# A retention, convolution and expert layer: the work ahead of the gather loop in another order

## The chip, the core and the metric

One NeuronCore of a Trainium2 chip runs the whole program. The metric is the device time of one execution in microseconds. TensorE is PE in the profile, VectorE is DVE, ScalarE is ACT, GpSimd is POOL, and SyncE is SP, which here only issues DMAs.

## The reference, cut to what matters

```python
h = rmsnorm(x)                                    # 512 prompt rows and 32 rows of running streams, D = 1024
q, k, v, g, a, b = split(h @ w_in)                # six sections of 512 columns
u = a * sigmoid(b)                                # gated
c = depthwise_conv(concat(conv_buf, u), 31 taps)  # per channel, 512 channels
y_conv = silu(layer_norm(c + bias) * gain + bias2)
o = retention(rotary(q), rotary(k), v, state)     # 4 heads of 128
y_ret = silu(g) * group_norm(o) * gain
x = x + concat(y_ret, y_conv) @ w_out
h = rmsnorm(x)
for each of 8 heads:                              # experts by product keys
    scores = (h @ query) against 2 x 128 keys; the best 16 of each; the best 16 of the 256 sums
    x += sum over 16 of softmax(best) * gelu(h . down[expert]) * up[expert]
y = rmsnorm(x)
```

Everything is in float32. `down` and `up` rows lie side by side, so an expert is one row of 8 KB.

## The kernel before

**Tiles.** The 544 rows are five tiles: four of 128 (tiles 0 to 3) and the sample tile of 32 (`SAMPLE`, tile 4). The 8 heads and the tiles make 34 virtual tiles (`VT`): for each head four of 128 rows, and the sample rows of all heads folded into two more. Each virtual tile gathers 16 experts for each of its 128 rows, 16 DMAs of 128 rows (`gathers`, L460), 544 in all.

**Front, on PE.** The normalised rows are transposed (`norm_t`, L1059). Sections A and B (`glu`) are computed channel-major: 32 pairs of products with 512 and with 32 columns each (L1077, L1082). Sections Q, K, G and V are row-major, one product of 8 matmuls for each tile (`qkvg`, L1090; a float32 matmul shows as two records). Then come the means and variances of the convolution's channels (`ln_mean`, `ln_var`, L1104), retention tile by tile (`ret_qT`, `ret_kT`, `ret_scores`, `ret_out`, `ret_state`, `ret_yT`), and the output product of each tile in two halves (`mix_out`, L1090 again). A weight section has 2 MB and a ring of three places in SBUF; SP loads the next when PE has drained the section whose place it takes.

**Front, on the others.** ACT empties the section products. DVE waits for all of section B and then computes 31 taps over four channel groups, each in a 512-column and a 32-column instruction, a drain after each tap (L728). GpSimd rotates q and k of a tile with twelve operations of 256 elements (L441 to L444); for tile 0 that starts when K's first product is in SBUF, which is during the taps. DVE copies the transposed heads, normalises retention's output with a root from GpSimd (`retention_root`, L424), and adds the output products to `xs` (`mix_add`, L833).

**Routing.** When a tile's two output halves are added, ACT squares it, GpSimd takes the root (`mixed_root`), DVE normalises (`peer_norm`, L853), PE turns it (`ffn_t`) and computes queries and scores (L1189, L1201), and DVE finds the best keys (`top_first`, `top_second`) and the experts (`top_sums`, L898, whose last line L918 releases the gathers). For head 0 this is done tile by tile in `TRANSITION`; later heads are done for all tiles at once beside the sums, from L1217 on.

**Expert loop.** The 11 ring places of gathered rows lie in the same SBUF as the weight ring and the sections' results, so the first gathers must wait until those are free. For each group of four experts DVE computes the dot products (`weigh`, L933), ACT makes gelu, weights and four diagonal matrices (L620 to L630), and PE sums the `up` rows through them (`sum_up`, L1246), which frees the four places.

**What sets the order.** Each engine's program is in order and written out by hand. PE's order is `retention_schedule` and `TRANSITION`. Each PE job has a PSUM bank, numbered round: seven banks, and three (4 to 6) from `ffn_t` of tile 2 on, because the sums use banks 0 to 3. A job waits until the engine that empties the former job of its bank has done so (`open_bank`, L1039; `BEFORE`).

## Time and profile before

| | us |
|---|---|
| median of 3 runs | 1797.5 (1796.53 to 1797.82) |
| the profiled execution | 1796.54 |
| its span in the trace | 1794.6 |
| PE busy | 1522.6 |
| DVE busy | 1171.6 |
| GpSimd busy | 744.8 |
| ACT busy | 496.4 |

The span is what the trace covers; the profiled execution's own time is 1.9 us longer. The page divides the span into 40 equal slices of 44.9 us. A busy PE is not PE at its peak, because matmuls are pipelined. PEclk is the granted clock as a share of 2.4 GHz.

### The profile page before, as it was taken

The numbers are of one execution on the slowest core, as the hardware profiler recorded it, in microseconds if no ns is written. First come the engines' busy times: TensorE is split into PE (matmuls) and PEld (weight loads), VectorE is DVE, ScalarE is ACT, GpSimd is POOL, SyncE is SP. The second block draws the span as 40 slices with busy tenths as digits, with TensorE's granted clock in tenths as the row PEclk, the third lists the DMA queues.
The fourth block names the chain that finished last, engine by engine and source line by source line (L and its number), as shares of the span: only waits on it lengthen the run. The fifth ranks groups of instructions, "written<-read, shape, count | busy, mean of one in ns | idle before, by whom it ended". The sixth has DMA issues, their size and how long they took to land.

```text
span 1794.6 us, 14135 instructions
## 1 busy us (share of the span) xinstructions
PE 1522.6 (85%) x4008; PEld 700.3 (39%) x4008; DVE 1171.6 (65%) x2667; ACT 496.4 (28%) x1562; POOL 744.8 (42%) x654
## 2 busy tenths in 40 slices
PE   7999979968988978997798889788977988777887
PEld 3544345534433433342244334333423443332332
DVE  2089863357567767766766777677677677777655
ACT  1000110122332333332333323333333332333332
POOL 1002144133254545453554544444454445455452
PEclk9899989989999999998999999999999999899899
DMA  5112100288999999999999999999999999999996
GB/s 221 47 58 83 62 1 1 68 341 329 362 404 421 421 421 421 422 421 422 421 402 423 422 420 401 422 421 389 408 422 421 421 421 422 421 421 410 421 416 248
DMA packets 84847, 605.53 MB, mean 337 GB/s; under 512 B 10880, under 2 KB 11136, under 8 KB 13088
## 3 DMA queue, kind: packets, MB, share of 16 engines
q0 software_dynamic: 78336, 570.46, 77.1%
q1 hardware_dynamic: 6432, 34.16, 5.0%
q8 instruction: 32, 0.52, 0.1%
q14 instruction: 47, 0.39, 0.1%
HBM read 601.31 MB, written 2.88 MB: 337 GB/s over the span
## 4 chain that ended last, share of the span: by engine, by line
DMA 39%; PE 38%; DVE 13%; ACT 4%; issue 2%; POOL 1%; DVEq 1%; ACTq 1%; POOLq 0%; SPq 0%
DMA arena<-experts,expert 38%; PE ps L1246 21%; DVE region_b L728 6%; PE ps L1217 5%; PE ps L1090 5%; DVE arena L933 5%; PE ps L1077 3%; ACT weight L623 2%; ACT diag L630 1%; PE ps L1082 1%; PE ps L1189 1%; POOL arena L465 1%; PE ps L1104 1%; ACT gl L620 1%; ACTq L625 1%
## 5 line engine op out<-in xcount | busy, mean ns | idle before, releaser
L1246 PE MATMUL ps<-arena,diag 128*128 128x512 f32 x2176 | 1031.2, 631 | 234.1 <-ACT diag L630 233.9
L465 POOL DMA_INDIRECT arena<-experts,expert x544 | 669.3, 1230 | 760.3 <-PE ps L1246 672.4
L933 DVE CUSTOM_DVE_ANT_0 arena<-arena,hn 128x1024 f32<-128x1024 f32 x544 | 654.8, 1222 | 365.9 <-DMA arena<-experts,expert 361.4
L1246 PEld LDWEIGHTS ps<-arena,diag 128*128 128x128 f32 x2176 | 428.8, 201 | 818.9 <-issue 603.4
L620 ACT ACTIVATE gl<-dots 128x4 f32<-128x4 f32 x136 | 27.9, 205 | 801.4 <-DVE dots L933 801.4
L630 ACT ACTIVATE diag<-cst,weight 128x128 f32<-128x128 f32 x544 | 173.8, 390 | 9.6 <-issue 0.3
L1090 PE MATMUL ps<-arena,hT 128*128 128x512 f32 (+1 forms) x320 | 145.9, 616 | 1.0 <-issue 1.0
L623 ACT ACTIVATE weight<-gl,gate 128x1 f32<-128x1 f32 x544 | 115.8, 283 | 9.9 <-issue 0.7
L728 DVE SCALAR_TENSOR_TENSOR region_b<-region_b,par 128x512 f32<-128x512 f32 x240 | 108.0, 521 | 2.7 <-issue 0.5
L1217 PE MATMUL ps<-hT,region_b 128*128 128x512 f32 x224 | 98.5, 593 | 0.4 <-issue 0.4
L441 POOL TENSOR_TENSOR hn<-arena,cst 128x256 f32<-128x256 f32 (+1 forms) x20 | 16.2, 808 | 193.5 <-ACT arena L529 127.0
L1090 PEld LDWEIGHTS ps<-arena,hT 128*128 128x128 f32 (+1 forms) x320 | 56.9, 181 | 86.8 <-issue 86.8
L1090 PE MATMUL ps<-arena,region_b 128*128 128x512 f32 (+1 forms) x160 | 70.5, 594 | 0.0
L1217 PEld LDWEIGHTS ps<-hT,region_b 128*128 128x128 f32 x224 | 42.5, 190 | 53.5 <-issue 53.5
L1077 PE MATMUL ps<-hT,arena 128*128 128x512 f32 x128 | 58.5, 619 | 2.8 <-DVE hT L707 2.5
L713 DVE SCALAR_TENSOR_TENSOR region_b<-region_b 128x512 f32<-128x512 f32 x4 | 2.5, 686 | 75.8 <-ACT region_b L517 75.8
L944 DVE TENSOR_TENSOR xs<-ps,xs 128x1024 f32<-128x1024 f32 (+1 forms) x34 | 41.4, 1219 | 15.3 <-PE ps L1246 15.3
L933 DVE DVE_READ_ACCUMULATOR2_ANT dots<- 128x1 f32 x544 | 44.5, 82 | 0.0
L620 ACT ACT_TABLE_LOAD x34 | 43.6, 1283 | 0.6
L606 ACT ACT_TABLE_LOAD x33 | 42.3, 1283 | 1.7
L1090 PEld LDWEIGHTS ps<-arena,region_b 128*128 128x128 f32 (+1 forms) x160 | 27.0, 174 | 36.8 <-issue 36.5
L529 ACT ACTIVATE arena<-ps 128x512 f32<-128x512 f32 (+1 forms) x15 | 8.9, 595 | 110.7 <-PE ps L1090 110.7
(125 smaller groups left out, 845.1 us busy)
## 6 DMA issues: line engine op xcount, KB each, us to landing
arena<-weights SPq DMA_DIRECT2D x8, 2048.0 KB, 8.9
...
arena<-experts,expert POOLq DMA_INDIRECT x544, 14.9
...
```

Source lines behind the costliest of these rows:

```text
L465: pool.indirect_dma_start(rows_of(n), None, experts, bass.IndirectOffsetOnAxis(ap=expert[:, vt % BUFS, k:k + 1], axis=0))\
L606: nc.scalar.activation(gate[:, u, :], best_s[:, u, :], ACT.Exp, bias=neg_max[:, u:u + 1], accum_out=gate_sum[:, u:u + 1]).then_inc(s_exp, 1)
L620: nc.scalar.activation(gl[:, vt % 2, ks], dots[:, vt % 2, ks], ACT.Gelu_apprx_tanh)
L623: nc.scalar.activation(weight[:, vt % 2, k:k + 1], gl[:, vt % 2, k:k + 1], ACT.Copy, scale=gate[:, vt % BUFS, k:k + 1])
L630: nc.scalar.activation(diag[:, n % DIAGS, :], base, ACT.Copy, scale=weight[:, vt % 2, k:k + 1])\
L728: last = v.scalar_tensor_tensor(out=out, in0=src[:, c, j:j + n], scalar=tap, in1=out, op0=ALU.mult, op1=ALU.add)
L933: last = v.tensor_tensor_reduce(out=rows_of(n)[:, 0:D], in0=rows_of(n)[:, 0:D], in1=hn[:, tile_of(vt)], scale=1.0, scalar=0.0, op0=ALU.mul ...
L944: v.tensor_tensor(out=xs[0:rows, tile], in0=total, in1=xs[0:rows, tile], op=ALU.add).then_inc(s_acc, 1)
L1077: last = mm(out, w[:, k, c * P:(c + 1) * P], hT[:, k, 0:SEQ], start=k == 0, stop=k == KD - 1)
L1090: last = mm(out[0:r, :], lhs[:, k, lo:lo + r], w[:, k, :], start=k == 0, stop=k == KD - 1)
L1217: last = mm(out, weights[:, k, i * KEYS:(i + 1) * KEYS], hT[:, k, 0:SEQ], start=k == 0, stop=k == KD - 1)
L1246: last = mm(ps[:, 2 * (vt % 2) + half, :], diag[:, n % DIAGS, :], rows_of(n)[:, D + half * SEC:D + (half + 1) * SEC], start=k == 0, stop=k ...
```

## The change

- PE's whole order, front and transition, is one list (`plan`). Sections A and B are computed in token halves of 272 columns, channel groups 0 and 1 first and then 2 and 3. Tile 3 and the sample tile are transposed after the first two half products. One product of G stands ahead of the means, one ahead of the variances, three behind them.
- The four channel groups' rows lie in one buffer of 604 columns, prompt and sample together, so a tap is one instruction of 574 columns. DVE does the 31 taps of groups 0 and 1, then those of groups 2 and 3, with a drain after each pair. The normalisation of the channels is done in two blocks of tokens, 128 and 416.
- GpSimd rotates in place, q and k together, six operations of 512 elements for a tile, after the last tap (`s_conv`), all tiles in a row.
- Retention, the output product and the routing of tile 0 come before the retention of tiles 2 to 4; the output products of the others follow. ACT instead of DVE copies the transposed heads and the turned-back output.
- PSUM: eight banks, and four (4 to 7) from `ffn_t` of tile 0 on.
- The ring places have another order, since gathers can start before the last sections are through; the number of places, 11, stays.
- SP issues the loads in another order: tile 3 and the sample rows behind section A; head 0's query weights when the taps are done; the gain of the second norm twice, once for tile 0 into its own place. The waits on PE's drains are waits on single PE jobs.

```diff
+EXT = PAD + SEQ + PAD + DEC
+WIDE = EXT - PAD
+HALF = T // 2
+BLOCKS = ((0, P), (P, T))
...
+    late = [(c, i) for c in (2, 3) for i in range(2)]
+    order = turn("norm_t", 0) + turn("norm_t", 1) + turn("norm_t", 2) + glu(S_A, (0, 0), (1, 0)) + turn("norm_t", 3)
+    order += turn("norm_t", SAMPLE) + glu(S_A, (0, 1), (1, 1)) + glu(S_B, (0, 0), (0, 1), (1, 0), (1, 1))
+    order += glu(S_A, *late) + glu(S_B, *late) + rows(S_Q, *range(TILES)) + rows(S_K, *range(TILES)) + rows(S_G, 0)
+    order += blocks("ln_mean") + rows(S_G, 1) + blocks("ln_var") + rows(S_G, 2, 3, SAMPLE)
+    order += rows(S_V, 0) + head(0) + rows(S_V, 1) + scores(0) + head(1) + out(0) + rows(S_V, 2) + scores(1) + back(0)
+    order += mix(0, 0) + out(1) + head(2) + mix(0, 1) + scores(2) + back(1) + rows(S_V, 3) + turn("ffn_t", 0)
+    order += query(0) + keys(0) + out(2) + head(3) + rows(S_V, SAMPLE) + scores(3) + mix(1, 0) + back(2) + mix(1, 1)
+    order += out(3) + head(4) + scores(4) + turn("ffn_t", 1) + query(1) + keys(1) + back(3) + out(4) + mix(2, 0)
+    order += back(4) + mix(2, 1) + sums(0, 0) + mix(3, 0) + turn("ffn_t", 2) + query(2) + mix(3, 1) + sums(0, 1)
+    order += keys(2) + mix(4, 0) + turn("ffn_t", 3) + query(3) + sums(0, 2) + mix(4, 1) + keys(3) + sums(0, 3)
+    return order + turn("ffn_t", 4) + query(4) + sums(1, 0) + keys(4) + sums(1, 1)
...
+BANKS = 8
+SUM_BANKS = 4
+Q_BANKS = SUM_BANKS
+FIRST_SUM = JOB[("ffn_t", 0, 0)]
+BANK = {name: n % BANKS if n < FIRST_SUM else SUM_BANKS + (n - FIRST_SUM) % (BANKS - SUM_BANKS)
+        for name, n in JOB.items()}
+BEFORE = {name: [other for other in JOBS[:n] if BANK[other] == BANK[name]][-1:] for name, n in JOB.items()}
...
+OPENING = [0, 1, 2, 3, 4, 5, 6, 0, 1, 2, 3, 7, 8, 9, 10]
+CYCLE = [4, 5, 6, 0, 1, 2, 3, 7, 8, 9, 10]
+SLOT = OPENING + [CYCLE[n % SLOTS] for n in range(VT * TOPK - len(OPENING))]
+PLACE = [6, 7, 4, 5, 8, 9, 10, 0, 1, 2, 3]
...
+            x_rows(0)
             sp.dma_start(cst[:, C_IDENT:], consts[:, C_IDENT:]).then_inc(s_ident, 16)
             sp.dma_start(par[:, :], params).then_inc(s_par, 16)
...
+            x_rows(1)
+            x_rows(2)
+            weight_rows(S_A)
+            x_rows(3)
+            x_rows(SAMPLE)
+            weight_rows(S_B)
+            weight_rows(S_Q)
+            sp.dma_start(u[:, :, PAD + SEQ:PAD + SEQ + PAD], conv_state).then_inc(s_st, 16)
+            sp.dma_start(state[:, 1], state_ret).then_inc(s_st, 16)
+            sp.dma_start(cst[:, 0:C_IDENT], consts[:, 0:C_IDENT]).then_inc(s_cst, 16)
+            sp.wait_ge(s_pe, JOB[("glu", S_A, CT - 1, 1)] + 1)
+            weight_rows(S_K)
+            sp.wait_ge(s_pe, JOB[("glu", S_B, CT - 1, 1)] + 1)
+            weight_rows(S_G)
+            sp.wait_ge(s_pe, JOB[("qkvg", S_Q, SAMPLE)] + 1)
+            weight_rows(S_V)
+            sp.wait_ge(s_u, 1)
+            sp.dma_start(conv_prompt, u[:, :, SEQ:SEQ + PAD]).then_inc(s_convout, 16)
+            sp.dma_start(conv_sample, u[:, :, EXT - PAD:EXT]).then_inc(s_convout, 16)
+            sp.wait_ge(s_pe, JOB[("qkvg", S_K, SAMPLE)] + 1)
+            weight_rows(S_OUT)
+            sp.wait_ge(s_convout, 32)
+            sp.wait_ge(s_conv, 1)
             sp.dma_start(head_flat[0], head_weights[0]).then_inc(s_hw[0], 16)
+            sp.wait_ge(s_pe, JOB[("qkvg", S_G, SAMPLE)] + 1)
+            weight_rows(S_OUT + 1)
+            sp.wait_ge(s_rot, TILES)
+            sp.dma_start(first_gain, gain_ffn.to_broadcast([P, D])).then_inc(s_gain1, 16)
+            sp.wait_ge(s_yconv, len(BLOCKS))
+            sp.dma_start(row_gain, gain_ffn.to_broadcast([P, D])).then_inc(s_gain, 16)
+            sp.wait_ge(s_by["dve"], EMPTIED[("ret_state", SAMPLE)])
...
+            def rotary(t):
+
+                r = ROWS[t]
+                pool.wait_ge(s_by["act"], EMPTIED[("qkvg", S_K, t)])
+                src = z[0:r, t, S_Q:S_K + 1].rearrange("p s (h d) -> p (s h) d", d=HD)
+                x1, x2 = src[:, :, 0:half], src[:, :, half:HD]
+                cos = trig[0:r, t, 0].unsqueeze(1).to_broadcast([r, 2 * HEADS, half])
+                sin = trig[0:r, t, 1].unsqueeze(1).to_broadcast([r, 2 * HEADS, half])
+                nc.gpsimd.tensor_tensor(out=rot[0][0:r], in0=x2, in1=sin, op=ALU.mult)
+                nc.gpsimd.tensor_tensor(out=rot[1][0:r], in0=x1, in1=sin, op=ALU.mult)
+                pool.drain()
+                nc.gpsimd.tensor_tensor(out=x1, in0=x1, in1=cos, op=ALU.mult)
+                nc.gpsimd.tensor_tensor(out=x2, in0=x2, in1=cos, op=ALU.mult)
+                pool.drain()
+                nc.gpsimd.tensor_tensor(out=x1, in0=x1, in1=rot[0][0:r], op=ALU.subtract)
+                nc.gpsimd.tensor_tensor(out=x2, in0=x2, in1=rot[1][0:r], op=ALU.add)
+                pool.drain().then_inc(s_rot, 1)
...
+            pool.wait_ge(s_cst, 16)
+            pool.wait_ge(s_conv, 1)
+            rotary(0)
+            decayed_keys(0)
+            for t in range(1, TILES):
+                rotary(t)
+            retention_root(0)
+            decayed_keys(1)
+            retention_root(1)
+            decayed_keys(2)
...
             mixed_root(0)
+            pool.wait_ge(s_idx, 1)
+            pool.wait_ge(s_pe, JOB[("ret_yT", 1)] + 1)
+            gathers(0, 0, 2)
+            retention_root(2)
+            decayed_keys(3)
+            pool.wait_ge(s_pe, JOB[("qkvg", S_V, SAMPLE)] + 1)
+            gathers(0, 2, 4)
+            pool.wait_ge(s_pe, JOB[("ret_yT", 2)] + 1)
+            gathers(0, 4, 5)
             mixed_root(1)
-            pool.wait_ge(s_idx, 1)
-            gathers(0, 0, 3)
+            retention_root(3)
+            decayed_keys(4)
+            pool.wait_ge(s_pe, JOB[("ret_yT", 3)] + 1)
+            gathers(0, 5, 6)
+            retention_root(4)
+            pool.wait_ge(s_pe, JOB[("ret_yT", 4)] + 1)
+            gathers(0, 6, 7)
             mixed_root(2)
-            pool.wait_ge(s_wsec, len(WEIGHT_ORDER) - 2)
-            gathers(0, 3, 7)
+            gathers(0, 7, 11)
             mixed_root(3)
-            pool.wait_ge(s_wsec, len(WEIGHT_ORDER))
-            gathers(0, 7, SLOTS)
+            pool.wait_ge(s_pe, JOB[("mix_out", SAMPLE, 0)] + 1)
+            gathers(0, 11, 13)
+            pool.wait_ge(s_pe, JOB[("mix_out", SAMPLE, 1)] + 1)
+            gathers(0, 13, TOPK)
             mixed_root(SAMPLE)
...
+            def glu_part(s, c, i):
+                name = ("glu", s, c, i)
+                func = ACT.Copy if s == S_A else ACT.Tanh
+                to = u[:, c, PAD:EXT] if s == S_A else conv[:, c, :]
+                filled(name)
+                if i == 0:
+                    emptied(nc.scalar.activation(to[:, 0:HALF], bank(name)[:, 0:HALF], func, scale=0.5))
+                else:
+                    nc.scalar.activation(to[:, HALF:SEQ], bank(name)[:, 0:SEQ - HALF], func, scale=0.5)
+                    emptied(nc.scalar.activation(to[:, SEQ + PAD:WIDE], bank(name)[:, SEQ - HALF:HALF], func, scale=0.5))
...
+            def turned_heads(t):
+                r = ROWS[t]
+                for kind, dst in (("ret_qT", qT), ("ret_kT", kT)):
+                    filled((kind, t))
+                    src = bank((kind, t)).rearrange("p (h n) -> p h n", h=HEADS)[:, :, 0:r]
+                    emptied(nc.scalar.activation(dst[:, :, 0:r], src, ACT.Copy))
...
-            mixed_squares(1)
+            turned_back(1)
+            rows_in(S_V, 3)
             turned_rows(0)
             first_query(0)
+            turned_heads(3)
+            rows_in(S_V, SAMPLE)
+            softmax(0)
+            turned_back(2)
+            mixed_squares(1)
+            turned_heads(4)
             turned_rows(1)
             first_query(1)
+            turned_back(3)
+            turned_back(4)
             mixed_squares(2)
-            mixed_squares(3)
-            softmax(0)
+            normalized(0)
+            group(0, 0)
             turned_rows(2)
             first_query(2)
+            mixed_squares(3)
+            group(0, 1)
+            turned_rows(3)
+            first_query(3)
+            group(0, 2)
             mixed_squares(SAMPLE)
-            head_tile(0, {0: lambda: turned_rows(3), 1: lambda: first_query(3), 3: lambda: turned_rows(4)})
+            softmax(1)
+            group(0, 3)
+            turned_rows(4)
...
+            def glu(c):
+                dve.wait_ge(s_by["act"], EMPTIED[("glu", S_B, c, 1)])
+                return v.scalar_tensor_tensor(out=u[:, c, PAD:EXT], in0=conv[:, c, :], scalar=1.0, in1=u[:, c, PAD:EXT],
+                                              op0=ALU.add, op1=ALU.mult)
+
+            def tap(c, j):
+                gain = par[:, G_TAPS + c * TAPS + j:G_TAPS + c * TAPS + j + 1]
+                if j == 0:
+                    return v.tensor_scalar(out=conv[:, c, :], in0=u[:, c, 0:WIDE], scalar1=gain,
+                                           scalar2=par[:, G_BIAS + c:G_BIAS + c + 1], op0=ALU.mult, op1=ALU.add)
+                return v.scalar_tensor_tensor(out=conv[:, c, :], in0=u[:, c, j:j + WIDE], scalar=gain,
+                                              in1=conv[:, c, :], op0=ALU.mult, op1=ALU.add)
...
+            normed(0)
+            normed(1)
+            dve.wait_ge(s_par, 16)
+            v.tensor_scalar(out=half_ln[:, :], in0=par[:, G_LNG:G_TAPS], scalar1=0.5, scalar2=None, op0=ALU.mult)
+            turned(0)
+            normed(2)
+            turned(1)
+            normed(3)
+            turned(2)
+            normed(SAMPLE)
+            turned(3)
+            turned(SAMPLE)
...
+            for first in range(0, CT, 2):
+                glu(first)
+                last = glu(first + 1)
+                if first + 2 == CT:
+                    last.then_inc(s_u, 1)
+                dve.drain()
+                for j in range(TAPS):
+                    for c in (first, first + 1):
+                        last = tap(c, j)
+                    if j < TAPS - 1:
+                        dve.drain()
+            last.then_inc(s_conv, 1)
             dve.wait_ge(s_cst, 16)
...
+            mean_off(0)
+            mean_off(1)
+            gated(0)
+            variance(0)
+            variance(1)
+            inverse_deviation(0)
+            conv_norm(0)
+            gated(1)
+            conv_silu(0)
+            inverse_deviation(1)
+            conv_norm(1)
+            gated(2)
+            gated(3)
+            gated(SAMPLE)
+            conv_silu(1)
+            ret_scores(0)
+            ret_out(0)
+            ret_state(0)
+            ret_scores(1)
+            mix_add(0, 0)
+            ret_out(1)
+            ret_state(1)
+            mix_add(0, 1)
+            ret_scores(2)
...
-            dve.wait_ge(s_gain, 16)
+            dve.wait_ge(s_gain1, 16)
             peer_norm(0)
-            mix_add(2, 0)
-            mix_add(3, 0)
-            dve.wait_ge(s_retout, 32)
+            dve.wait_ge(s_rot, TILES)
+            dve.drain()
             first_scores(0)
             top_first(0)
+            top_second(0)
+            top_sums(0)
+            ret_out(2)
+            ret_state(2)
+            ret_scores(3)
+            mix_add(1, 0)
+            mix_add(1, 1)
+            ret_out(3)
+            ret_state(3)
+            ret_scores(4)
+            dve.wait_ge(s_gain, 16)
             peer_norm(1)
-            top_second(0)
-            mix_add(4, 0)
-            top_sums(0)
-            mix_add(2, 1)
             first_scores(1)
             top_first(1)
+            ret_out(4)
+            ret_state(4)
+            top_second(1)
+            mix_add(2, 0)
+            top_sums(1)
+            mix_add(2, 1)
+
+            gate_scales(0)
+            weigh(0, 0)
+            mix_add(3, 0)
             peer_norm(2)
             mix_add(3, 1)
-            top_second(1)
-            mix_add(4, 1)
-            top_sums(1)
-            peer_norm(3)
-
-            gate_scales(0)
-            weigh(0, 0)
+            weigh(0, 1)
             first_scores(2)
             top_first(2)
-            weigh(0, 1)
+            mix_add(4, 0)
+            peer_norm(3)
+            weigh(0, 2)
             top_second(2)
-            weigh(0, 2)
-            peer_norm(4)
+            mix_add(4, 1)
             top_sums(2)
             weigh(0, 3)
+            peer_norm(4)
+            first_scores(3)
 
             gate_scales(1)
             weigh(1, 0)
-            first_scores(3)
...
+            def glu_part(s, c, i):
                 w = section(s)
...
+                out = open_bank(("glu", s, c, i))
+                for k in range(KD):
+                    last = mm(out[:, 0:HALF], w[:, k, c * P:(c + 1) * P], hT[:, k, i * HALF:(i + 1) * HALF],
+                              start=k == 0, stop=k == KD - 1)
+                done(last)
...
             def mix_out(t, i):
...
                 if i == 0:
...
+                    pe.wait_ge(s_yconv, 2 if t else 1)
+                    pe.wait_ge(s_by["act"], EMPTIED[("ret_yT", t)])
+                rows_times(("mix_out", t, i), yT, section(S_OUT + i), ROWS[t], t * P)
```

## Rows read from the trace of the kernel before

**Rows 1.** The page's 40 slices: DMA share in tenths and GB/s moved.
```profile
DMA  5112100288999999999999999999999999999996
GB/s 221 47 58 83 62 1 1 68 341 329 362 404 421 421 421 421 422 421 422 421 402 423 422 420 401 422 421 389 408 422 421 421 421 422 421 421 410 421 416 248
```

**Rows 2.** Windows: us, busy us (count) per engine, PEclk, DMA share, GB/s.
```profile
15.00:20.00 5.00, 2.48 (x19) 1.75 (x18) 4.01 (x9) 0.00 (x0) 0.00 (x0) 1.00 1.07 421
...
400.00:420.00 20.00, 12.50 (x48) 7.36 (x48) 18.90 (x46) 3.20 (x14) 3.91 (x4) 0.83 0.62 220
...
420.00:1794.00 1374.00, 1149.99 (x2784) 511.81 (x2784) 940.66 (x2128) 443.71 (x1458) 654.32 (x535) 0.95 0.99 410
...
460.00:480.00 20.00, 19.94 (x47) 8.97 (x48) 9.58 (x17) 4.21 (x11) 5.07 (x5) 1.00 0.91 360
```

**Rows 3.** Timeline: start us, us, engine, line; the squares of tile 3, PE's sections.
```profile
9.48 1.06 ACT L495 ACTIVATE hn<-xs 128x1024 f32<-128x1024 f32 x1 [0.69 <-DMA xs<-x_prompt]
...
19.07 27.73 PE L1077 MATMUL ps<-hT,arena 128*128 128x512 f32 x64 [2.52 <-DVE hT L707]
46.64 9.02 PE L1082 MATMUL ps<-hT,arena 128*128 128x32 f32 x64
...
86.48 8.01 PE L1082 MATMUL ps<-hT,arena 128*128 128x32 f32 x64
...
132.09 34.69 PE L1090 MATMUL ps<-arena,hT 128*128 128x512 f32 x80 [0.26 <-issue]
```

**Rows 4.** DVE: timeline; taps by form in 157 to 207, then 139.9 to 154.
```profile
94.84 2.50 DVE L713 SCALAR_TENSOR_TENSOR region_b<-region_b 128x512 f32<-128x512 f32 x4 [75.82 <-ACT region_b L517]
...
111.28 99.73 DVE L728 SCALAR_TENSOR_TENSOR region_b<-region_b,par 128x512 f32<-128x512 f32 x216 [0.49 <-issue]
...
L728 DVE SCALAR_TENSOR_TENSOR region_b<-region_b,par 128x512 f32<-128x512 f32 x59 | 44.0, 746 | 1.0
L728 DVE SCALAR_TENSOR_TENSOR region_b<-region_b,par 128x32 f32<-128x32 f32 x58 | 14.2, 244 | 0.0
...
L728 DVE SCALAR_TENSOR_TENSOR region_b<-region_b,par 128x512 f32<-128x512 f32 x10 | 9.2, 918 | 0.2
```

**Rows 5.** Timeline of GpSimd: a 512-element operation beside the taps, and later.
```profile
152.53 1.37 POOL L451 TENSOR_TENSOR hn<-hn,cst 128x512 f32<-128x512 f32 x1 [0.24 <-issue]
...
246.33 1.04 POOL L451 TENSOR_TENSOR hn<-hn,cst 128x512 f32<-128x512 f32 x1
```

**Rows 6.** Timeline of PE from 268 to 461 us.
```profile
268.65 9.51 PE L1090 MATMUL ps<-arena,hT 128*32 128x512 f32 x16
...
348.70 3.84 PE L1189 MATMUL ps<-hT,region_b 128*128 128x128 f32 x32 [0.74 <-ACT hT L560]
...
359.69 14.02 PE L1090 MATMUL ps<-arena,region_b 128*128 128x512 f32 x32
...
387.73 9.77 PE L1246 MATMUL ps<-arena,diag 128*128 128x512 f32 x16 [8.12 <-ACT diag L630]
...
438.08 7.13 PE L1246 MATMUL ps<-arena,diag 128*128 128x512 f32 x16 [2.04 <-ACT diag L630]
...
460.06 7.10 PE L1217 MATMUL ps<-hT,region_b 128*128 128x512 f32 x16 [0.36 <-issue]
```

**Rows 7.** Timeline of DVE: tile 0's scores, its experts, tile 0's first four rows.
```profile
339.86 0.41 DVE L862 COPY region_b<-ps 128x256 f32<-128x256 f32 x1
...
352.70 0.17 DVE L918 SCALAR_TENSOR_TENSOR expert<-picked 128x16 uint32<-128x16 f32 x1
...
381.31 1.21 DVE L933 CUSTOM_DVE_ANT_0 arena<-arena,hn 128x1024 f32<-128x1024 f32 x1
...
385.87 0.08 DVE L933 DVE_READ_ACCUMULATOR2_ANT dots<- 128x1 f32 x1
```

**Rows 8.** GpSimd's first gather (timeline), and all 544 of line 465 to landing.
```profile
353.18 1.20 POOL L465 DMA_INDIRECT arena<-experts,expert  x1 [28.62 <-DVE expert L918]
...
DMA to landing us min/median/max: 5.4/14.9/20.6
```

577 lines of the change are left out of this document (245 added, 332 removed).

## The prediction

> **What bounds the kernel now.** I read the page's slices first. From the tenth slice on the DMA engines are busy in nine tenths or more and move some 421 GB/s; before that they are almost idle [rows 1]. From 420 us to 1794 us they are busy in 0.99 of the time at 410 GB/s [rows 2]. So there are two parts: a front of some 420 us which the compute engines set, and a gather loop which memory sets. 544 gathers of 1.05 MB at 421 GB/s are 2.49 us each, 1355 us. Nothing of the change alters the loop. What counts is when the loop reaches the state it has today, and the front's own length is only worth what it moves that moment.
>
> The second reading is the tensor engine's timeline. It stands in a closed row from 19 us: section A until 55.7, section B until 94.5, then 6.94 us for each product of a tile with a section [rows 3]. The vector engine idles until 94.84, runs the taps until 210.9 [rows 4], and the first routing ends at 352.87 [rows 7]. The last output product ends at 373.7 [rows 6]. Tile 0's four sums then begin at 387.7, and after stops of up to 8 us the tensor engine is in a closed row again from 454 to 507 (sums, head 1's queries). In it DMA falls to 0.91 [rows 2]. My yardstick is therefore the first product of head 1, at 460.06 [rows 6]: the tensor engine bounds this place, and after it the program is unchanged.
>
> **Start and gated sections.** Tile 3's rows are moved behind section A (2.1 MB) on SP's queue. Now they arrive at 9.48 [rows 3]; 2.1 MB at 421 GB/s are 5 us [rows 2], and with the constants ahead I take 15.3. Squares, root, normalising and turning need 4.6, and the vector queue has tile 3's normalising ahead of tile 2's turn, so the sections start at 19.9, not 19.07. A 512-column record is 27.73/64 = 0.433 us; 272 columns are 0.230, and 256 of them 58.9 us, against 75.5 now with the 32-column records [rows 3]: 16.6 less. The first half of them (29.5) and the turns of tiles 3 and 4 (2.9) end at 52.3; with 0.6 for the tanh the vector engine starts at 52.9, not 94.84.
>
> **Convolution.** A tap on 512 columns lasts 0.746 and on 32 columns 0.244 [rows 4]; eight of them overlap by some 0.085 each and with a drain of 0.17 make the tap's 3.46. 574 columns are then 0.727 from start to start, a pair with its drain 1.62. 62 pairs and the gating are 103.2 us: done at 156.1 instead of 210.9. The rotation of tile 0 sits inside the taps now; there the 512-column row reads 0.918 [rows 4]. Moved behind the taps, this goes. The tensor engine ends the sections at 81.8 and then does Q, K and one product of G, 11 x 6.94: it reaches the means at 158.1. The two are level, 53 us ahead of today.
>
> **Until tile 0 is routed.** Means 3.9, G 6.9, variances 3.7, G 20.8, V 6.9: 200.3. All this covers the vector engine's normalisation (some 25 us with waits for ScalarE) and the five rotations: 30 operations of 1.04 [rows 5] and drains, 36 us, ready by 197. Then five products (34.7) and the small steps of retention, turning and query (20: turns near 1, scores near 1, out and state 1.8 to 2.7, query 3.84 [rows 6], two short waits): tile 0's scores stand at 255. Copy to experts takes 13.0 less 2.95 for what stands between, 10.1 [rows 7]: routed at 265.3 instead of 352.9, **88 us earlier**.
>
> **Why little of it is left.** Five steps give it back. First, the V product of the sample tile. From tile 0's turn on only banks 4 to 7 rotate, so a job needs the bank of the job four before it, and four before this product stands ret_out(2). The vector engine empties that bank, in a step that is now queued behind the whole routing of tile 0; its root is on GpSimd behind two gathers of some 1.2 us [rows 8]. Gathers until 268.1, root 1.5, norm 1.4: the bank is free at 271.1. The tensor engine has nothing left at 258.6 (after out(2) and head(3)), so 12.5 us are new idle time, and a product after a stop reads 9.51 for 6.94 [rows 6]: done at 280.5. Before, this step had no routing in front of it.
>
> Second, scores(3), two products, out(3), state and head(4) last until 299.2. scores(4) needs ret_out(3)'s bank, whose root stands behind tile 1's on GpSimd (302.2); then come peer_norm(1), turn and query 1, back(3), out(4), mix(2,0), mix(2,1): 330.9. The vector engine adds and weighs four rows in 4.6 [rows 7], until 336.5, ScalarE makes the diagonals 1.75 later: sums(0,0) at 338.2. After a stop of that length it is 9.6 long today [rows 6]: 347.8.
>
> Third, a circle: mix(3,0) to 354.7. Only then can the vector engine add and normalise tile 2 (2.1); turn and query last until 362.9, mix(3,1) until 369.8; weigh(0,1) is queued behind its add, so sums(0,1) runs from 377 to 385.9.
>
> Fourth, the same circle for tile 3 and the sample tile: keys, mix(4,0) to 393.3, peer_norm(3), query to 401.6, sums(0,2) to 410.8, mix(4,1) to **417.7**, against 373.7 now [rows 6]. Up to then only 13 gathers have a place to land.
>
> Fifth, gathers 13 to 15 need the ring rows of the last output section: issued at 417.8, the first lands 5.4 later [rows 8], the others 2.49 apart, the third at 428.5. weigh(0,3) ends at 429.7, sums(0,3) runs from 431.4 to 440.2 (today sums(1,0) already begins at 438.1 [rows 6]), turn and query of the sample tile until 445.6, sums(1,0) and (1,1) with keys until 460.3. Gather 27 lands at 458.4, before its use at 470, so memory does not bound this stretch.
>
> Head 1's first product comes at 460.3, against 460.06 today [rows 6]. In this stretch of 14 hand-offs I charged the stops of over 3 us with slow clock, the product of V 2.6, sums(0,0) 2.7, sums(0,1) and (0,3) 2.0 each, 9.3 together; two shorter ones (turn and query of tiles 2 and 3) may cost about 1 each: 462. **Sum: 1796.5 + 2 = 1798.5** against the profiled execution (span 1794.6). That one stands 1.0 below the median of the runs, so 1799 as a median.
>
> Costed at nothing: the new order of the ring places (the same number of gathers in flight, 11), ScalarE's copies of turned heads in place of the vector engine's (ScalarE is busy 3 of 20 us there), the tensor engine's drains that go (0.26 us each), the second read of the norm's gain (512 KB while memory is almost idle [rows 1]). None of them stands on the chain above; if the copies did, each would add 0.6 to the retention steps.
>
> Unknown prices and their ends. Clock after a stop: nothing (6.94) to 2.9 us (387.73's 9.77) [rows 6]; I took 2 to 3 where the stop is over 3 us. Rotation on 512 elements beside vector work: 1.04 to 1.37 each [rows 5], 36 to 46 us, both covered until 208. Section A's arrival: 9.5 (no delay) to 20 us; I took 15.3, since the queue's rate is shown. Half sections: 58.9 by columns, up to 64 if a record keeps part of its 0.43.
>
> **Rivals.** Faster. The stops cost no clock: the 9.3 charged and the 2 added go, 1787. For it: the stop of 2.04 before 438.08 is followed by a full-speed row, 7.13 [rows 6]. Against: 9.51 and 9.77 after longer ones, and most new stops are long. Chance 0.28.
>
> Slower. One place: the end of mix(4,1). From about 417 on, each microsecond it comes late makes the whole kernel one later, as the last three gathers of tile 0 and all of tile 1's hang on it. It lies behind three circles in which the tensor engine waits for an add, the add for a product. If four more of its short stops cost the full 2.9, it ends near 429: 1810. For it: clock 0.83 from 400 to 420 [rows 2], where such circles run today. Chance 0.26.
>
> Rotation. Two-input vector operations beside GpSimd got 0.17 longer on average [rows 4]. If each of the normalisation's some 25 operations stood still for one whole GpSimd operation (1.04), the vector engine would be free at 213, not by 208, and tile 0's scores and all behind them 5 late: 1804. Chance 0.05. The Trainium skill, SBUF — State Buffer, section Who interferes with whom, states just this: the shared port pair is an exclusive lock held for an instruction, and a vector instruction with two SBUF inputs contends with a GpSimd one that reads SBUF. By this rule the conv block and the rotations, now put side by side, slow each other; the rows beside the taps agree in direction.
>
> The front doesn't matter at all, the loop finds its old place whatever comes: 1797.5. Chance 0.03.
>
> **How the numbers follow.** The forecast's own case has 0.38 and lies in 1793 to 1805, as single terms err by a few us: of it 0.03 below 1793.9, 0.25 within, 0.10 above 1801.1. About 0.2% (3.6 us) is what a measurement of this kernel can tell from no change. Faster 0.03 + 0.28 = 0.31; same 0.25 + 0.03 = 0.28; slower 0.10 + 0.26 + 0.05 = 0.41. The range reaches into both side cases: 1785 to 1812.
>
> **What would show it.** Right: first tap near 53, taps done near 156, means near 158, experts of tile 0 near 265; a V product of the sample tile waiting some 12 us until 271 for the vector engine; the last output product ending at 415 to 420; DMA at full rate only from about 420; head 1's first product at 458 to 465. Wrong, if the V product does not wait; if the taps end past 165; if sums(0,3) is over before 430 (faster) or begins after 440 (slower); or if the loop after 510 runs at another rate than 421 GB/s.

## The result, and the profile after

| | before | after |
|---|---|---|
| median, us | 1797.0 (1793.6 to 1797.8, 4 runs) | 1821.3 (1820.9 to 1824.5, 4 runs) |
| ratio to before | | 1.0144, 95% interval 1.0128 to 1.0160 |
| span of the profiled run | 1794.6 | 1819.1 |

The change makes the kernel 24 us slower, 1.4%. I had forecast 1799 us in a range of 1785 to 1812, with slower (0.41) only a little ahead of faster (0.31): the measured time lies above the range.

The page's slices of after, beside [rows 1]:

```profile
DMA  5211112316899999999999999999999999999995
GB/s 218 93 49 73 70 44 76 147 46 257 361 373 421 422 421 421 421 421 422 421 396 408 422 421 414 422 420 406 416 421 422 415 421 422 420 422 412 408 423 237
```

A slice is 45.5 us. From the thirteenth, some 546 us, the gathers move 421 GB/s without a dip for eight slices; the three before it read 257, 361 and 373. Windows of after (columns as in [rows 2]):

```profile
360.00:380.00 20.00, 12.96 (x51) 7.71 (x52) 5.27 (x9) 3.87 (x13) 2.51 (x2) 0.86 0.00 0
...
400.00:420.00 20.00, 15.58 (x47) 7.61 (x47) 3.14 (x11) 2.72 (x10) 1.26 (x2) 0.87 0.29 105
420.00:440.00 20.00, 5.07 (x14) 1.77 (x13) 12.85 (x28) 6.54 (x16) 11.68 (x12) 0.73 0.77 314
440.00:460.00 20.00, 19.63 (x69) 10.46 (x68) 8.72 (x21) 3.16 (x13) 6.65 (x6) 0.85 1.01 379
460.00:480.00 20.00, 8.95 (x24) 3.94 (x22) 13.60 (x35) 6.44 (x22) 8.74 (x6) 0.92 1.02 423
480.00:500.00 20.00, 18.63 (x37) 8.22 (x38) 10.45 (x20) 4.21 (x11) 3.79 (x4) 0.82 0.73 286
```

From 460 to 480 us PE is busy for 8.95 us, and memory pays for it 20 us later: 0.73 of its time, since rows that are not summed keep their places: GpSimd issues no gather from 474 to 493.3 us, when a sum of PE frees a place. PE's timeline in the front:

```profile
19.65 9.21 PE L1224 MATMUL ps<-hT,arena 128*128 128x272 f32 x32 [5.80 <-DVE hT L812]
...
158.68 4.05 PE L1240 MATMUL ps<-region_b,ones_cw 128*128 128x128 f32 x16
...
200.90 1.04 PE L1213 MATMUL ps<-cst,arena 128*128 128x128 f32 x8
```

Up to here all is as forecast (sections 19.9, means 158.1, last V of the front 200.3). So is the first stop; then the circles, tile 0's sums (L1361) and the last output product (L1231 at 416.52):

```profile
270.49 9.53 PE L1231 MATMUL ps<-arena,hT 128*32 128x512 f32 x16 [12.50 <-DVE hn L923]
...
340.78 8.60 PE L1361 MATMUL ps<-arena,late 128*128 128x512 f32 x16 [7.14 <-ACT late L720]
...
377.75 8.91 PE L1361 MATMUL ps<-arena,late 128*128 128x512 f32 x16 [6.99 <-ACT late L720]
...
397.88 5.46 PE L1301 MATMUL ps<-hT,region_b 128*128 128x128 f32 x32 [0.74 <-ACT hT L650]
407.76 8.83 PE L1361 MATMUL ps<-arena,late 128*128 128x512 f32 x16 [4.42 <-ACT late L720]
416.52 7.05 PE L1231 MATMUL ps<-arena,region_b 128*32 128x512 f32 x16
...
439.14 8.93 PE L1361 MATMUL ps<-arena,late 128*128 128x512 f32 x16 [14.93 <-ACT late L720]
...
464.56 7.13 PE L1361 MATMUL ps<-arena,late 128*128 128x512 f32 x16 [2.74 <-ACT late L720]
```

And the row that decides, head 1's first product, in the same timeline:

```profile
481.37 9.98 PE L1329 MATMUL ps<-hT,region_b 128*128 128x512 f32 x16 [9.68 <-issue]
```

It starts 21.3 us later than in before (460.06, [rows 6]) and lasts 2.9 longer: 24.2 of the 24.5 us by which the spans differ. "Issue" says only that the profile names no releaser. The code names two: ScalarE's copy of the sample tile's query and VectorE's copy of its scores (`first_scores(4)`, L1009). VectorE's timeline:

```profile
474.37 1.23 DVE L1076 CUSTOM_DVE_ANT_0 arena<-arena,hn 128x1024 f32<-128x1024 f32 x1 [1.25 <-DMA arena<-experts,expert]
475.52 0.08 DVE L1076 DVE_READ_ACCUMULATOR2_ANT dots<- 128x1 f32 x1
475.52 0.42 DVE L1014 MAX8 best_s<-rot_tmp 128x8 f32<-128x256 f32 x1
...
480.96 0.18 DVE L1061 SCALAR_TENSOR_TENSOR expert<-picked 128x16 uint32<-128x16 f32 x1
481.06 0.22 DVE L1009 COPY region_b<-ps 128x64 f32<-128x64 f32 x1
```

A copy of 0.22 us, whose scores PE had finished at 461.8, stands behind a weigh that waits for the row of gather 27 (474.37) and behind `top_sums(3)` (5.5 us). Before, the same copy was made as soon as PE had the scores (VectorE's timeline of the kernel before):

```profile
459.73 0.23 DVE L866 COPY region_b<-ps 128x64 f32<-128x64 f32 x1 [1.93 <-PE ps L1180]
```

### The profile page after: what moved, and what is told of

The parts are those of the page before. It is cut to its first block, busy times and chain, and to the rows that moved or that the text cites. A ratio compares the mean times of both kernels' runs of the same rounds, so it can differ in the third digit from the quotient of the medians.

```text
span 1819.1 us, 14057 instructions
## 1 busy us (share of the span) xinstructions
PE 1519.1 (84%) x4008; PEld 714.2 (39%) x4008; DVE 1164.0 (64%) x2539; ACT 508.5 (28%) x1603; POOL 743.1 (41%) x624
## 4 chain that ended last, share of the span: by engine, by line
PE 44%; DMA 41%; DVE 6%; ACT 4%; issue 3%; POOL 1%; ACTq 1%; DVEq 0%; SPq 0%; POOLq 0%
DMA arena<-experts,expert 41%; PE ps L1361 20%; PE ps L1231 12%; PE ps L1329 5%; DVE arena L1076 4%; PE ps L1224 3%; ACT weight L713 2%; ACT late L720 1%; PE ps L1301 1%; POOL arena L499 1%; DMA xs<-x_prompt 1%; ACT gl L710 1%; ACTq L715 1%; PE ps L1213 0%; PE ps L1240 0%
## 5 line engine op out<-in xcount | busy, mean ns | idle before, releaser
L1361 PE MATMUL ps<-arena,late 128*128 128x512 f32 x2176 | 1041.3, 636 | 241.3 <-ACT late L720 241.2
L1361 PEld LDWEIGHTS ps<-arena,late 128*128 128x128 f32 x2176 | 432.5, 203 | 833.7 <-issue 614.0
L720 ACT ACTIVATE late<-cst,weight 128x128 f32<-128x128 f32 x544 | 173.9, 390 | 9.7 <-issue 0.3
L1231 PE MATMUL ps<-arena,hT 128*128 128x512 f32 (+1 forms) x320 | 141.9, 602 | 12.5 <-DVE hn L923 12.5
L838 DVE SCALAR_TENSOR_TENSOR region_b<-region_b,par 128x574 f32<-128x574 f32 x120 | 92.6, 814 | 4.5
L1231 PEld LDWEIGHTS ps<-arena,hT 128*128 128x128 f32 (+1 forms) x320 | 55.2, 175 | 95.2 <-issue 95.1
L1231 PE MATMUL ps<-arena,region_b 128*128 128x512 f32 (+1 forms) x160 | 70.6, 594 | 1.3 <-issue 1.3
L1224 PE MATMUL ps<-hT,arena 128*128 128x272 f32 x256 | 60.8, 401 | 6.5 <-DVE hT L812 6.5
L455 POOL TENSOR_TENSOR rot_tmp<-arena,cst 128x512 f32<-128x512 f32 (+1 forms) x5 | 6.6, 1313 | 137.0 <-DVE region_b L838 136.5
L1224 PEld LDWEIGHTS ps<-hT,arena 128*128 128x128 f32 x256 | 49.6, 194 | 17.4 <-DVE hT L812 7.0
L949 DVE TENSOR_TENSOR xs<-ps,xs 128x512 f32<-128x512 f32 (+1 forms) x10 | 6.9, 689 | 75.3 <-PE ps L1231 75.3
L1231 PEld LDWEIGHTS ps<-arena,region_b 128*128 128x128 f32 (+1 forms) x160 | 27.1, 174 | 38.7 <-issue 38.4
```

The lines of the kernel that those rows point to most:

```text
L720: nc.scalar.activation(diag[:, n % DIAGS, :], base, ACT.Copy, scale=weight[:, vt % 2, k:k + 1])\
L838: return v.scalar_tensor_tensor(out=conv[:, c, :], in0=u[:, c, j:j + WIDE], scalar=gain, in1=conv[:, c, :], op0=ALU.mult, op1=ALU.add)
L1224: last = mm(out[:, 0:HALF], w[:, k, c * P:(c + 1) * P], hT[:, k, i * HALF:(i + 1) * HALF], start=k == 0, stop=k == KD - 1)
L1231: last = mm(out[0:r, :], lhs[:, k, lo:lo + r], w[:, k, :], start=k == 0, stop=k == KD - 1)
L1361: last = mm(ps[:, 2 * (vt % 2) + half, :], diag[:, n % DIAGS, :], rows_of(n)[:, D + half * SEC:D + (half + 1) * SEC], start=k == 0, stop=k ...
```

## The experiments

Ratios are to the kernel before, with 95% intervals; differences between kernels are differences of medians, good to some 3 us (5 for run 2, whose four times lie 9 us apart). "The changed kernel" is the kernel after the change, at 1821.3. A theory is one of those in the expectation above the result, and what is measured decides between them.

**1. The sample tile's scores earlier on VectorE.**

```diff
             top_second(3)
+            first_scores(4)
             weigh(1, 2)
             top_sums(3)
-            first_scores(4)
             weigh(1, 3)
```

> Edit: on VectorE the copy and search of the sample tile's scores (first_scores(4)) stand ahead of weigh(1,2) and top_sums(3) instead of behind them. Theory 1, queue place: head 1's first product waits 9.68 us only for a copy that is queued on VectorE behind a weigh whose last row lands at 474.4; moved ahead, the copy is made by about 465, the product starts at 471.8 instead of 481.4 and reads 7.1 instead of 10.0, and the whole kernel is 8 to 13 us faster than the changed kernel (about 1808 to 1813). Theory 2, memory: from 440 us on the DMA engines are busy in 1.01 and 1.02, so the gathers are what is late, and the product that starts earlier only waits for rows further on: 0 to 3 us faster (1818 to 1821), head 1's product at 472 all the same.

Measured 1809.8 us, ratio 1.0071 (1.0054 to 1.0088): 11.5 us faster than the changed kernel. The wait in front of head 1's first product is gone from PE's timeline:

```profile
467.55 7.11 PE L1361 MATMUL ps<-arena,late 128*128 128x512 f32 x16
474.50 7.03 PE L1329 MATMUL ps<-hT,region_b 128*128 128x512 f32 x16
```

Theory 1 holds. The product comes 6.9 us earlier and is 2.9 shorter, 9.8 of the 11.5. It is not at the 471.8 I had expected, as the output products ended 2.4 us later in this profile.

**2. Eight banks until tile 1's turn.**

```diff
-FIRST_SUM = JOB[("ffn_t", 0, 0)]
+FIRST_SUM = JOB[("ffn_t", 1, 0)]
```

> Edit: all eight PSUM banks rotate until tile 1's turn instead of tile 0's turn, so the sample tile's V product no longer needs the bank that VectorE empties only behind the routing of tile 0. Theory 1, the delay passes on one to one: the 12.5 us wait before that product and its slow clock (9.5 for 6.9) go, out(3) and all behind it come 12 to 15 us earlier, the last output product ends at 409 to 412 instead of 423.6, and the kernel is 10 to 15 us faster (1806 to 1811). Theory 2, absorbed: VectorE, GpSimd and the circles of tiles 2 and 3 set the later steps anyway (retention_root(2) stays behind the two first gathers on GpSimd, and out(2)'s normalising stays behind the routing), so the wait only moves to the next job that needs that result: 0 to 4 us faster (1817 to 1821), with a new wait of some 10 us before the output products of tile 2.

Measured 1811.7 us, ratio 1.0073 (1.0053 to 1.0093): 9.5 us faster, just below theory 1's 10 to 15 and far from theory 2's 0 to 4. Two rows of PE's timeline, the V product and the last output product:

```profile
259.42 7.05 PE L1231 MATMUL ps<-arena,hT 128*32 128x512 f32 x16
...
409.03 7.05 PE L1231 MATMUL ps<-arena,region_b 128*32 128x512 f32 x16
```

The V product ends 13.5 us earlier, the last output product 7.5. Part of the gain is lost to a new wait of 5.07 us for `peer_norm(1)` before tile 1's turn (290.90; it was 2.66) and to slower rows behind the stops (sums(0,0) to (0,2) read 10.12, 9.97 and 9.73 for 8.60, 8.91 and 8.83). The 9.68 us in front of head 1's first product are still there, at 474.

**3. Both.** The two diffs above together.

> Edit: both of the two former edits, early scores of the sample tile on VectorE and eight banks until tile 1's turn. If both losses are in series, as I hold: the gains add, 20 to 27 us faster than the changed kernel, 1794 to 1801, level with the kernel before. If memory sets the stretch from 440 to 480 us: the earlier end of the output products brings the gathers 13 to 15 forward by 10 and the sum is the second edit's gain alone, 10 to 15 us. If the second edit's gain is absorbed: the first edit's gain alone, 8 to 13 us.

Measured 1797.2 us, ratio 1.0009 (0.9999 to 1.0018): 24.1 us faster than the changed kernel. The two add up (11.5 and 9.5, within the noise). Head 1's first product starts at 458.94 and reads 7.03, the span is 1794.1; before had 460.06 and 1794.6. One copy earlier and another numbering of the banks undo the whole loss, but the output products still end at 410.6, not at 373.7.

**4. The rotations beside the taps, on the changed kernel.**

```diff
             pool.wait_ge(s_cst, 16)
-            pool.wait_ge(s_conv, 1)
             rotary(0)
```

> Edit: the wait of GpSimd for the last tap (s_conv) is left out, so the rotations run as soon as q and k of a tile are there, beside VectorE's taps. Theory 1: rotations of 512 elements beside taps slow both, the 574-column taps read over 0.9 us instead of 0.81 while they overlap, some 25 of the 62 pairs are hit, the taps end 5 to 12 us later than 155.4 and the means start as much later; the start of the routing of tile 0 and the end of the kernel move by the same amount, 5 to 12 us slower (1826 to 1833). Theory 2: the early front has slack (the rotations are ready earlier, V and retention wait for less), so the end moves by less than half of what the means move.

Measured 1851.8 us, ratio 1.0301 (1.0284 to 1.0318): 30.6 us slower, far more than I expected. VectorE's two pairs of channel groups, the first without and the second with rotations beside it (from the two timelines of this kernel, VectorE's and PE's):

```profile
55.66 48.45 DVE L837 SCALAR_TENSOR_TENSOR region_b<-region_b,par 128x574 f32<-128x574 f32 x60
...
106.69 77.05 DVE L837 SCALAR_TENSOR_TENSOR region_b<-region_b,par 128x574 f32<-128x574 f32 x60
```

```profile
183.80 5.50 PE L1239 MATMUL ps<-region_b,ones_cw 128*128 128x128 f32 x16 [25.17 <-DVE region_b L837]
```

The rotations run from 124.8 to 178.3. In these 53.5 us the taps lose 28.6, and a rotation's operation takes 1.6 to 1.8 us on average by line, against 1.3 to 1.4 behind the taps. By the Trainium skill, SBUF — State Buffer, section Who interferes with whom, a VectorE instruction with two SBUF inputs and a GpSimd instruction that reads SBUF contend; here both sides of that rule show, with the numbers of the last sentence. The means come 25.1 us later, head 1's product 30.8 later (512.13), the end 30.6: nothing behind absorbs a delay of the front. Theory 1 is right in kind, at some three times its price (the means 5 to 12 us later); theory 2 falls.

**5. The output products first** (on top of run 3). PE's list:

```diff
-    order += back(4) + mix(2, 1) + sums(0, 0) + mix(3, 0) + turn("ffn_t", 2) + query(2) + mix(3, 1) + sums(0, 1)
-    order += keys(2) + mix(4, 0) + turn("ffn_t", 3) + query(3) + sums(0, 2) + mix(4, 1) + keys(3) + sums(0, 3)
+    order += back(4) + mix(2, 1) + mix(3, 0) + sums(0, 0) + turn("ffn_t", 2) + mix(4, 0) + mix(3, 1) + sums(0, 1)
+    order += mix(4, 1) + query(2) + sums(0, 2) + keys(2) + turn("ffn_t", 3) + query(3) + sums(0, 3) + keys(3)
```

VectorE: weigh(0,0), peer_norm(2), mix_add(3,0), weigh(0,1), mix_add(4,0), mix_add(3,1), weigh(0,2), peer_norm(3), mix_add(4,1), peer_norm(4), weigh(0,3), and the routing of tiles 2 and 3 behind that. ScalarE and GpSimd have the same steps in the order in which these produce them; on GpSimd the gathers 11 and 12 now stand ahead of `mixed_root(3)`.

> Edit, on top of the two former ones (early scores of the sample tile, eight banks until tile 1's turn): the output products of tile 3 and the sample tile come ahead of the sums and queries of tile 0 to 2 that stood between them, on all engines' lists, so that no product waits for an add that is queued behind a weigh (the circles of my third and fourth step). Theory 1, the circles cost: the last output product ends near 362 us instead of 410.6, the gathers 13 to 15 are used by about 375 instead of 423, memory is at its full rate from about 365, head 1's first product comes near 405 to 425 instead of 459, and the kernel is 30 to 50 us faster than the one with the two edits (1797.2), so 1747 to 1767 and faster than the kernel before. Theory 2, tensor engine full: its work between 320 and 460 us (some 85 us of products, queries and sums) was only spread by the waits, and head 1's products then wait for gathers, whose 544 x 2.49 us count from a start that moves little: 0 to 15 us faster, 1782 to 1797.

Measured 1753.8 us, ratio 0.9754 (0.9728 to 0.9780): 43.4 us faster than run 3, and 2.5% faster than before. PE's timeline, from the two output products of tiles 2 and 3 in one row to head 1's first product:

```profile
313.35 14.00 PE L1231 MATMUL ps<-arena,region_b 128*128 128x512 f32 x32
327.62 7.10 PE L1361 MATMUL ps<-arena,late 128*128 128x512 f32 x16 [0.28 <-ACT late L720]
...
356.45 7.05 PE L1231 MATMUL ps<-arena,region_b 128*32 128x512 f32 x16
...
385.16 5.95 PE L1301 MATMUL ps<-hT,region_b 128*128 128x128 f32 x32 [9.70 <-ACT hT L650]
...
418.95 7.03 PE L1329 MATMUL ps<-hT,region_b 128*128 128x512 f32 x16
```

The last output product ends at 363.5 instead of 410.6, head 1's first comes at 419.0 instead of 458.9. Theory 1: the waits, not the work, filled the stretch. The edit moves many steps at once, so its 43 us are the worth of the whole order. They include most of the wait in front of sums(0,2) (6.09 us in run 3), in which a row waits for gather 11, because that gather's issue on GpSimd falls from 5.93 to 0.94 us here. The wait of 9.70 us is new: on ScalarE the turned rows of tile 3 stand behind group(0,3), which waits for gather 15.

**6. And the ring places.** As run 5, with the places that tile 0's sums free used before those of the last output product:

```diff
-OPENING = [0, 1, 2, 3, 4, 5, 6, 0, 1, 2, 3, 7, 8, 9, 10]
-CYCLE = [4, 5, 6, 0, 1, 2, 3, 7, 8, 9, 10]
+OPENING = [0, 1, 2, 3, 4, 5, 6, 0, 1, 2, 3, 7, 8, 4, 5, 6, 9, 10]
+CYCLE = [0, 1, 2, 3, 7, 8, 4, 5, 6, 9, 10]
```

> Edit: as the last one, and the ring places that tile 0's sums free (4, 5, 6) are used again before those that the last output product frees (9, 10), so the gathers 13 to 15 no longer wait for the last output product. Theory 1, the three gathers are what holds the loop: they are issued at 350 to 355 instead of 362 to 367, and the end comes 5 to 10 us earlier than without it. Theory 2, the tensor engine holds the loop by then (its row is closed from 362 us on): below 3 us.

Measured 1744.6 us, ratio 0.9704 (0.9680 to 0.9728): 9.1 us faster than run 5 (theory 1), 53.8 faster than the before kernel measured beside it, and the best kernel here. GpSimd's order changes with it: the gathers 11 to 15 stand ahead of `mixed_root(3)`, and tile 1's first two ahead of `mixed_root(SAMPLE)`; how much of the 9.1 us is theirs was not tried apart. The last output product, the wait in front of tile 3's query, and head 1's first product on PE:

```profile
356.32 7.05 PE L1233 MATMUL ps<-arena,region_b 128*32 128x512 f32 x16
...
376.72 3.84 PE L1303 MATMUL ps<-hT,region_b 128*128 128x128 f32 x32 [1.39 <-ACT hT L652]
...
410.06 7.03 PE L1331 MATMUL ps<-hT,region_b 128*128 128x512 f32 x16
```

The gathers 13 to 15 went out at 351.5 to 355.9 instead of 363.8 to 366.4. From 327.8 to 450 us PE never waits longer than 1.4 us.

**7. The output products first, alone.** Run 5's order on the changed kernel, without runs 1 and 2.

> Edit: the output products of tile 3 and the sample tile ahead, as before, but on the changed kernel itself: the V product of the sample tile still waits for its bank, and the sample tile's scores are still copied behind weigh(1,2) and top_sums(3). If the three losses are in series (V's bank 14.6, the scores' place 14.6, the circles 43.4 us by the former runs), this kernel is 43 us faster than the changed one, 1778. If the late scores are hidden by the new order (the weigh before them then waits for rows that land earlier), 52 to 58 faster, 1763 to 1769. If the gain of the order needs the two others, under 35 faster, above 1786.

Measured 1768.1 us, ratio 0.9851 (0.9831 to 0.9872): 53.2 us faster than the changed kernel, the second case. V's bank still costs (12.50 us of wait; run 5, which has runs 1 and 2 in it, is 14.4 faster). The late scores cost next to nothing: the copy is made at 431.52, right when sums(1,1) has ended.

```profile
431.84 7.10 PE L1329 MATMUL ps<-hT,region_b 128*128 128x512 f32 x16 [0.57 <-issue]
```

Here the last row of weigh(1,2) starts at 424.80 without waiting for memory. In these runs the copy's place costs time only where that row comes late.

**8. Throwaway products in six waits, on the changed kernel.**

```diff
+            def throwaway(b, n):
+                for _ in range(n):
+                    mm(ps[:, b, :], ones_cw[:, :], cst[:, C_CROSS:C_CROSS + SEC], start=True, stop=True)
```

> Edit, on the changed kernel: in six waits of the tensor engine (the V product of the sample tile, the four sums of tile 0, head 1's first product) it computes 4 to 15 products whose results are written over by the next real one. Nothing else moves. Theory 1, the stops cost clock and that is on the path: the products behind the waits read about 7.0 instead of 9.53, 8.60, 8.91, 8.83, 8.93 and 9.98 us, the last output product ends 6 to 9 us earlier, and the kernel is 8 to 14 us faster (1807 to 1813). Theory 2, the clock's cost is hidden in the next wait: the rows are shorter but the end moves by less than 3 us (1818 or more). Theory 3, the throwaway products run at the slow clock themselves and end behind the wait they should fill: no gain or a loss of some us.

Measured 1813.7 us, ratio 1.0102 (1.0082 to 1.0121): 7.6 us faster. There were 13 of them before the V product, 7, 7, 4 and 15 before the sums, 9 before head 1's product. PE's timeline (L1383 are the throwaway products, here those before head 1's):

```profile
270.73 7.03 PE L1232 MATMUL ps<-arena,hT 128*32 128x512 f32 x16 [1.34 <-DVE hn L924]
...
434.96 8.83 PE L1362 MATMUL ps<-arena,late 128*128 128x512 f32 x16 [2.08 <-ACT late L721]
...
466.25 7.89 PE L1383 MATMUL ps<-cst,ones_cw 128*128 128x512 f32 x18
476.09 8.80 PE L1330 MATMUL ps<-hT,region_b 128*128 128x512 f32 x16 [1.95 <-issue]
```

Four of the six rows fall from between 8.6 and 9.5 us to 7.0 or 7.1; the two where I left 2 us of wait still read 8.8 (8.93 and 9.98 in the changed kernel). The last output product ends at 419.4, 4.2 us earlier. The gain is just below theory 1's 8 to 14 and clear of theory 2: the clock's cost is on the path. It is less than runs 1 and 7 gave, and not clear of run 2's 9.5. (The throwaway rows themselves read 7.89 us for 18 records, full speed: theory 3 falls.)

**9. The rotations beside the taps, on the fastest kernel.** The diff of run 4 on run 6.

> Edit, on the fastest kernel so far (1744.6): GpSimd rotates beside the taps, as in the fourth run, where the means came 25.1 us later and the kernel got 30.6 us slower. Theory 1, the early front is worth its full length once the transition has no waits: 25 to 32 us slower, 1770 to 1777. Theory 2, with memory at its full rate from 350 us on, part of the delay is taken up by the tensor engine's slack: under 15 us slower.

Measured 1771.9 us, ratio 0.9869 (0.9852 to 0.9887): 27.3 us slower than run 6, with the means at 185.28. Theory 1: the front's delay of 25 us reaches the end in full here too, as it did in run 4.

**10 and 11. Loads beside the gathers, on the changed kernel.** Run 10 repeats the load of the last norm's gain; run 11 moves it and the sample rows' copies behind the load of head 3's weights.

```diff
-            for j in range(1, FOLDED):
-                sp.dma_start(hn[j * DEC:(j + 1) * DEC, SAMPLE, :], hn[0:DEC, SAMPLE, :]).then_inc(s_rep, 16)
-            sp.dma_start(row_gain, gain_final.to_broadcast([P, D])).then_inc(s_gain2, 16)
...
                 sp.dma_start(head_flat[head % 2], head_weights[head]).then_inc(s_hw[head % 2], 16)
+                if head == 3:
...
```

> Edit, on the changed kernel: the load of the last norm's gain (512 KB to 128 partitions, at 440.6 us) is done nine times, each behind the one before, and nothing else moves: 4.2 MB more, 10 us at 421 GB/s, from about 442 to 480 us. Theory 1, memory bounds this stretch (my forecast said it does not): the gathers 20 to 31 share the DMA engines with it, the last row of weigh(1,2) lands 4 to 9 us later than at 474.4, head 1's first product comes as much later than 481.4, and the kernel is 6 to 12 us slower than the changed one (1827 to 1833). Theory 2, the gathers have slack there: product and end move by less than 2 us.

> Edit, on the changed kernel: the copies of the sample tile's normalised rows (3 x 128 KB) and the load of the last norm's gain (512 KB), which run from 439 to 445 us beside the gathers, are issued behind the load of head 3's weights instead. Theory 1, memory bounds the stretch: 0.9 MB less is 2.2 us at 421 GB/s, and up to 4 us if they run at a lower rate (the slices at 445 us read 280 GB/s); weigh(1,2) ends and the product starts 2 to 4 us earlier, the kernel is 1 to 4 us faster (1817 to 1820), as the loads fall later into a stretch in which memory is the bound too: the sum may well be 0. Theory 2: no row moves by more than 0.5 us.

Run 10: 1825.8 us, ratio 1.0166 (1.0134 to 1.0199), which overlaps the changed kernel's interval. It does not decide: the eight added loads were issued only from 456 us on, some 8 us apart, and in that profile the transition is 2.7 us late before any of them (head 1's weights at 426.28 for 423.60). The last row of weigh(1,2) comes at 476.86, 2.5 us later, so one or two added loads delayed it by nothing that can be seen, which speaks against theory 1 as far as it goes. Run 11: 1817.5 us, ratio 1.0120 (1.0088 to 1.0151), again overlapping the changed kernel's. Its rows tell more, as it has its last output product where the changed kernel has it (the load behind it is issued at 423.39 against 423.60). The last row of weigh(1,2), the product, and the window 440 to 460:

```profile
468.95 1.23 DVE L1077 CUSTOM_DVE_ANT_0 arena<-arena,hn 128x1024 f32<-128x1024 f32 x1 [2.99 <-DMA arena<-experts,expert]
```

```profile
475.96 9.14 PE L1330 MATMUL ps<-hT,region_b 128*128 128x512 f32 x16 [7.13 <-issue]
```

```profile
440.00:460.00 20.00, 19.63 (x69) 10.45 (x69) 12.77 (x30) 5.45 (x23) 6.85 (x6) 0.85 1.01 420
```

Row and product come 5.4 us earlier, and the window moves 420 GB/s instead of 379. With those loads out of the stretch the row comes earlier, so memory does bound it. The 5.4 us are more than the 2.2 that 0.9 MB take at 421 GB/s, and more than theory 1's 4. Which of the loads slows the gathers stays open: the repeated gain load of run 10 showed no such effect (419 GB/s from 460 to 480), the copies of the sample rows were not tried alone. The end gained at most part of the 5.4 (3.8 by the medians, hardly clear of the noise).

## Why the prediction was wrong

**What held.** The front within 2 us (taps from 54.7, means 158.7, tile 0's experts at 264.6, 88 us earlier); the V product's stop (12.5 us, then 9.53 long, at 270.5 for 271.1); the circles; and the yardstick, since head 1's first product carries 24.2 of the 24.5 us. The rotations took 42.9 us (155.5 to 198.4), not 36: one of their operations reads 1.26 with nothing beside it, and the 1.04 of [rows 5] belongs to the decayed keys, another operation. That was within the bounds given (36 to 46) and covered. The rotation rival at 0.05 did not come: beside the rotations four 128-column operations of VectorE took 3.82 us together (1.11 in run 4, where nothing ran beside them), but the last block was done at 205.6, in time. In the changed kernel rotations beside the taps would cost 28.6 us (run 4), far more than the 0.918 of [rows 4] suggests. That the 512-element operations and 574-column taps are the reason was not tested.

**The step that failed: the fifth.** "Gather 27 lands at 458.4, before its use at 470, so memory does not bound this stretch." Both halves were wrong: its use had to wait for it, at 474.37. For gather 15 VectorE's timeline reads

```profile
436.23 1.23 DVE L1076 CUSTOM_DVE_ANT_0 arena<-arena,hn 128x1024 f32<-128x1024 f32 x1 [1.27 <-DMA arena<-experts,expert]
```

- Of the 16.0 us between 458.4 and 474.37, 7.7 were there already: gather 15 was used at 436.23, not at 428.5. 6.0 of these are the late end of the last output product (below), the rest lies between issue and landing of gather 13 (used 7.4 us after its issue, not 5.4). The other 8.3 are the rate: 12 gathers in 38.1 us are 3.18 each, not 2.49. I counted only gathers; in the window 420 to 480 SP's loads (head 1's and 2's weights, the sample rows, the gain) move 3.28 of 22.3 MB. Run 11 gives 5.4 back.
- I took its use for weigh(1,2) alone. Queued behind that weigh was VectorE's copy of the sample tile's scores, for which head 1's first product waits. So the gather's lateness became PE's: 9.68 us of stop and 2.9 of clock. Run 1 takes them away, 11.5 us. I had asked of each added wait what is queued behind it, but not of a wait (weigh for its row) that was there before and got longer.

**The fourth step, under-sized by 5.9.** The last output product ended at 423.6, not 417.7. Up to mix(4,0) the chain was 0.8 us late (394.1 for 393.3): the query of tile 1 took 6.67 us for 3.84, but sums(0,0) read 8.60 where 9.6 was charged. Then sums(0,2) began at 407.8. The forecast has it end at 410.8 at full clock, so begin near 404. It waited for the row of gather 11:

```profile
404.84 1.23 DVE L1076 CUSTOM_DVE_ANT_0 arena<-arena,hn 128x1024 f32<-128x1024 f32 x1 [5.42 <-DMA arena<-experts,expert]
```

That gather's issue on GpSimd took 5.93 us instead of 0.95. PE stopped 4.42 us for it and the sum read 8.83, not 6.94. These 6.3 us are an estimate of what the long issue cost; it was not tried alone. The slower rival named this place, for another reason (four more short stops at the full 2.9, to 429). Its rule that each microsecond late there makes the kernel one later fits roughly: run 3 against run 1 ends the last output product 15.3 us earlier and the kernel 12.6.

**The sum.** The forecast had sums(1,1) end at 460.3; it ended at 471.7, 11.4 later: the 7.7 of gather 15, then sums(1,0) at 8.81 for 6.94, a stop of 2.74 before sums(1,1), and small steps that were 0.9 shorter. Add the 9.68 us of the stop before head 1's product and its 2.9 of clock, and take off the 1.7 that was charged on top of 460.3: 22.3 us, which is 1821.3 less 1799.0. (The forecast's 1798.5 and 1.0 are 1799.5, given as 1799.)

**Where the 88 us went.** The fourth step named it, and run 5 shows the size: 43 us lay in the order of the transition, in which output products waited for adds queued behind weighs (and sums(0,2) for gather 11). Some 10 to 14 lay in V's bank (runs 2 and 7), 11.5 in the place of one copy (run 1; nothing once the new order is in). These overlap; measured together are run 3's 24 and run 5's 43 on top of it. With all of it and the ring mended (run 6) the changed front is some 53 us ahead of before. In that kernel PE has hardly a wait from 327 to 450 us, so it is the bound there. Whether before's own order could be mended in the same way wasn't tried, so no run says how much of the 53 us needs the early front; run 9 shows only that giving back some 25 us of it costs 27.
